# Transposed decay, update and attention matrices in a gated-delta-rule scan

## The reference

```python
decay = exp(where(incl, cum[:, None] - cum[None, :], -inf))
t_mat = where(strict, beta[:, None] * (k @ k.T) * decay, 0) + eye(c)      # I + L
sol   = triangular_solve(t_mat, [k * beta * exp(cum), v * beta])          # w_c, u_c
v_new = u_c - w_c @ s
o     = (q * exp(cum)) @ s + ((q @ k.T) * decay) @ v_new
s     = s * exp(cum[-1]) + (k * exp(cum[-1] - cum)).T @ v_new
```

## Time and profile before

| | before |
|---|---|
| median time | 2821.73 us |
| span of the profiled execution | 2811.5 us |
| busy: TensorE / VectorE / ScalarE / GpSimd | 2659.4 / 1589.4 / 1005.1 / 561.9 us |
| scan of layer 0 | from about 273 to 517 us of the span |
| scan of layer 1 | from about 1811 to 2033 us of the span |

### The profile page before, as it was taken

The page is one execution under the profiler, slowest core; times in us unless marked ns, Lnnn a source line. Parts: engine busy times, 40 slices in busy tenths (PEclk is TensorE's granted clock), DMA queues, the critical chain, the costliest instruction groups (busy, mean ns, idle before and its releaser), DMA issues.

```text
span 2811.5 us, 50275 instructions
## 1 busy us (share of the span) xinstructions
PE 2659.4 (95%) x21222; PEld 2123.3 (76%) x21222; DVE 1589.4 (57%) x2784; ACT 1005.1 (36%) x1642; POOL 561.9 (20%) x232
## 2 busy tenths in 40 slices
PE   7899999999999999999999989899899999999998
PEld 1388778888888888887787538777778787888676
DVE  4846677527554443435747764667637754352856
ACT  0335444322222343224532234454343333432542
POOL 0122000120113211321023512200031132242132
PEclk9999999999999999999999999999999999999999
DMA  8421000332222112220034552100053331231133
GB/s 261 150 69 44 20 23 22 108 116 98 79 87 90 61 53 100 80 91 27 31 120 147 194 190 75 46 26 25 25 186 114 101 109 57 92 125 61 35 117 116
DMA packets 95166, 250.97 MB, mean 89 GB/s; under 512 B 11010, under 2 KB 28804, under 8 KB 94432
## 3 DMA queue, kind: packets, MB, share of 16 engines
q1 hardware_dynamic: 84170, 219.56, 23.1%
q10 hardware_dynamic: 10774, 28.19, 2.8%
HBM read 205.12 MB, written 35.26 MB: 85 GB/s over the span
## 4 chain that ended last, share of the span: by engine, by line
PE 74%; DVE 15%; ACT 4%; issue 3%; DMA 3%; ACTq 0%; SPq 0%; DVEq 0%
PE ps L983 18%; PE ps L984 17%; PE ps L985 17%; PE ps L1570 4%; PE ps L991 4%; PE ps L1597 2%; PE ps L1000 2%; PE ps L1123 2%; DVE t_gcv L2280 1%; PE ps L1012 1%; DMA t_raw<-in_w_ada 1%; PE ps L1580 1%; PE ps L1077 1%; PE ps L1594 1%; PE ps L1169 1%
## 5 line engine op out<-in xcount | busy, mean ns | idle before, releaser
L944 POOL TENSOR_TENSOR t_wlo<-t_raw,t_whi 128x1024 fp32r<-128x1024 f32 x217 | 535.1, 2467 | 2178.5 <-ACT t_whi L1703 2178.5
L983 PE MATMUL ps<-t_u_hi,t_whi 128*128 128x512 f32 (+1 forms) x2368 | 862.6, 364 | 16.9 <-issue 5.4
L984 PE MATMUL ps<-t_u_lo,t_whi 128*128 128x512 f32 (+1 forms) x2368 | 834.4, 352 | 0.3 <-issue 0.3
L985 PE MATMUL ps<-t_u_hi,t_wlo 128*128 128x512 f32 (+1 forms) x2368 | 830.4, 351 | 0.0
L1703 ACT ACTIVATE t_whi<-t_raw 128x1024 fp32r<-128x1024 f32 x235 | 248.2, 1057 | 793.7 <-PE ps L985 680.2
L983 PEld LDWEIGHTS ps<-t_u_hi,t_whi 128*128 128x128 f32 x2368 | 449.6, 190 | 89.3 <-issue 19.7
L985 PEld LDWEIGHTS ps<-t_u_hi,t_wlo 128*128 128x128 f32 x2368 | 447.9, 189 | 63.5
L984 PEld LDWEIGHTS ps<-t_u_lo,t_whi 128*128 128x128 f32 x2368 | 449.7, 190 | 57.1 <-issue 3.3
L2903 DVE TENSOR_REDUCE t_amx<-ps 128x1 f32<-128x768 f32 (+1 forms) x120 | 101.5, 846 | 150.3 <-PE ps L1570 149.8
L1774 ACT ACTIVATE t_grp<-ps 128x512 f32<-128x512 f32 (+2 forms) x236 | 103.8, 465 | 221.4 <-PE ps L1000 103.0
L2280 DVE SCALAR_TENSOR_TENSOR t_gcv<-ps,t_par,t_gcv 128x511 f32<-128x511 f32 (+1 forms) x132 | 82.9, 628 | 106.1 <-ACT t_gcv L1774 102.1
(11 more groups left out here) (301 smaller groups left out, 3840.4 us busy)
## 6 DMA issues: line engine op xcount, KB each, us to landing
t_raw<-in_w_in SPq DMA_DIRECT2D x184, 512.0 KB, 3.6
t_raw<-in_w_ada SPq DMA_DIRECT2D x48, 512.0 KB, 4.5
t_raw<-in_w_br SPq DMA_DIRECT2D x32, 512.0 KB, 3.9
t_raw<-in_w_out SPq DMA_DIRECT2D x24, 512.0 KB, 4.4
t_sg<-gate_logits SPq DMA_DIRECT2D x28, 384.0 KB, 4.5
hs<-t_hstage ACTq DMA_DIRECT2D x20, 512.0 KB, 3.6
t_hring<-hs SPq DMA_DIRECT2D x20, 512.0 KB, 5.6
t_prob<-t_pT ACTq DMA_DIRECT2D x56, 128.0 KB, 2.1
```

Of the source, the lines that this page charges most:

```text
L944: pool.tensor_tensor(lo, raw[:, s % RAW, :], hi.bitcast(f32), ALU.subtract)\
L983: pe.matmul(o, lh, rh, start=first, stop=False)
L984: pe.matmul(o, lh, rl, start=False, stop=False)
L985: return pe.matmul(o, ll, rh, start=False, stop=last)
```

## The change

Everything that was formed as a matrix B is now formed as its transpose. The decay matrix, M and the attention matrix come out of the products in the orientation in which TensorE wants them as its stationary operand, and so `turn_m`, `turned_m` and the transposes of the attention matrix, with their copies, are gone. For this the factor beta goes to the columns: it is in the attention matrix and in k_tail, v enters unscaled (`beta_v` is gone), and q's norm moves from the attention matrix to the output (`within_chunk` on VectorE: one addition over 512 columns becomes four multiply-adds of 128 columns). `first_y` now fills Y with the masked copies and `first_x` transposes it into X; `first_q` waits for X. M, X and Y lie in two buffers in turn (`scan_m`, `scan_x`, `scan_y`). Two small VectorE operations a direction are added ahead of the scan.

```diff
+        def scan_m(t, d):
+            return grp[:, d, 2, :] if t % 2 else m_buf[:, d, :]
+        def scan_x(t, d):
+            return grp[:, d, 3, 256:512] if t % 2 else grp[:, d, 3, 0:256]
+        def scan_y(t, d):
+            return grp[:, d, 3, 0:256] if t % 2 else grp[:, d, 3, 256:512]
...
-                def turn_m():
-                    for d in range(2):
-                        ln.take("g_m")
-                        claim(3 * d)
-                        ln.done(turn(3 * d, m_buf[:, d, :]), "g_mt")
-                        lend("g_mt_ok", 3 * d)
-
-                def first_q():
+                def first_q(t):
                     for d in range(2):
-                        ln.take("g_mt_ok")
-                        ln.take("g_x0")
+                        ln.take("g_m")
+                        ln.take("g_y")
                         claim(3 * d + 1)
...
                 def within_chunk(d):
-                    ln.take("g_at_ok")
+                    ln.take("g_a")
...
-                            if t + 1 < NT:
-                                turn_m()
...
-                        if lv == 2:
-                            for d in range(2):
-                                if outs[d]:
-                                    ln.take("g_a")
-                                    claim(3 * d)
-                                    ln.done(turn(3 * d, grp[:, d, 0, :]), "g_at")
-                                    lend("g_at_ok", 3 * d)
...
-                def turned_m():
-                    for d in range(2):
-                        ln.take("g_mt")
-                        ln.done(run(grp[:, d, 2, :], ps[:, 3 * d, :], ACT.Copy), "g_mt_ok")
...
-                def beta_v(t):
...
                         for d in range(2):
-                            step(tt(dirs(gsc[:, 3, :], d), dirs(ec[:, 2 * d, :], d), dirs(gsc[:, 1, :], d), ALU.mult))
+                            step(ts(dirs(gsc[:, 3, :], d), dirs(ec[:, 2 * d, :], d), -1.0, None, ALU.mult))
+                            tail = dirs(ec[:, 2 * d + 1, :], d)
+                            step(tt(tail, tail, dirs(gsc[:, 0, :], d), ALU.mult))
...
-                def first_x(d):
+                def first_y(t, d):
                     ln.take("g_pre")
-                    x = by_head(grp[:, d, 3, 0:256])
+                    y = by_head(scan_y(t, d))
                     for r in near:
-                        last = dve.copy_predicated(x[r], over_heads(masks[r, d, 0, :]), by_head(m_buf[:, d, :])[r, :, r])
-                    ln.step(last, "g_x0")
-
-                def first_y(d):
-                    ln.done(dve.transpose(grp[:, d, 3, 256:512], grp[:, d, 3, 0:256]), "g_y")
+                        last = dve.copy_predicated(y[r], over_heads(masks[r, 1 - d, 0, :]), by_head(scan_m(t, d))[r, :, r])
+                    step(last)
+
+                def first_x(t, d):
+                    ln.done(dve.transpose(scan_x(t, d), scan_y(t, d)), "g_y")
...
                         ln.take("g_oa")
-                        ln.step(tt(gtok[:, c, :], ps[:, 6, :], gtok[:, c, :], ALU.add), "g_o2")
+                        ln.step(each(lambda h, s: stt(gtok[:, c, s], ps[:, 6, s],
+                                                      ssq[:, 2, c * HEADS + h:c * HEADS + h + 1],
+                                                      gtok[:, c, s], ALU.mult, ALU.add)), "g_o2")
...
                                 ln.take("g_ks")
-                                ln.take("g_pre")
                                 ln.done(each(lambda h, s: stt(grp[:, d, 0, s], ps[:, 3 * d + 2, s],
-                                                              gsc[:, 3, i0 + h:i0 + h + 1], grp[:, d, 0, s],
+                                                              gsc[:, 3, i0 + h:i0 + h + 1], vtok[:, c, s],
                                                               ALU.mult, ALU.add)), "g_r")
```

More of the change, by code:

```diff
@@ L1268, in decays @@
                         claim(3 * d)
-                        ln.done(pe.matmul(ps[:, 3 * d, :], cst[:, C_GE if d else C_LE, :], m_buf[:, d, :],
+                        ln.done(pe.matmul(ps[:, 3 * d, :], cst[:, C_LT if d else C_GT, :], scan_m(t, d),
                                           start=True, stop=True), "g_d")
@@ L1303, in gdn_scan @@
                 k_by_k(0)
-                turn_m()
-                first_q()
+                first_q(0)
                 for t in range(NT):
@@ L1314, in gdn_scan @@
                             claim(B + 1)
-                            ln.done(blocks(B + 1, grp[:, d, 2, :], grp[:, d, 3, :], d if lv == LEVELS - 1 else None, True,
-                                           lv),
+                            ln.done(blocks(B + 1, scan_m(t, d), scan_x(t, d), d if lv == LEVELS - 1 else None, True, lv),
                                     "g_q")
@@ L1334, in gdn_scan @@
                             ln.take("g_q_ok")
-                            ln.take("g_y")
+                            if lv > 1:
+                                ln.take("g_y")
                             if lv < LEVELS - 1:
                                 claim(B + 2)
-                                ln.done(blocks(B + 2, grp[:, d, 3, 256:512], grp[:, d, 5, :], lv=lv), "g_p")
+                                ln.done(blocks(B + 2, scan_y(t, d), grp[:, d, 5, :], lv=lv), "g_p")
                                 lend("g_x", B + 2)
@@ L1343, in gdn_scan @@
                             claim(B + 1)
-                            ln.done(blocks(B + 1, grp[:, d, 5, :], grp[:, d, 3, 256:512],
+                            ln.done(blocks(B + 1, grp[:, d, 5, :], scan_y(t, d),
                                            1 - d if lv == LEVELS - 1 else None), "g_pt")
@@ L1382, in gdn_scan @@
                     if t + 1 < NT:
-                        first_q()
+                        first_q(t + 1)
                     for d in range(2):
@@ L1961, in k_tail @@
                                 lambda h: ec[:, 2 * d + 1, c * 8 + d * 4 + h:c * 8 + d * 4 + h + 1], "g_ktail")
-                identities()
+                identities(0)
                 decays()
-                turned_m()
                 q_of(0, 1)
                 for t in range(NT):
-                    outs = [l == 0 or chunk(t, d) < LT for d in range(2)]
                     for lv in range(1, LEVELS):
@@ L1976, in gdn_scan @@
                         yield
[L1977 to L1981, removed]
                         if lv == 3 and t + 1 < NT:
@@ L2632, in gdn_scan @@
                             if lv <= IN_DVE:
-                                ln.step(dve.transpose(grp[:, d, 3, 256:512], grp[:, d, 3, 0:256]), "g_y")
+                                ln.step(dve.transpose(scan_y(t, d), scan_x(t, d)), "g_y")
                                 continue
@@ L2671, in gdn_scan @@
                         for d in range(2):
-                            first_x(d)
+                            first_y(t + 1, d)
                     for d in range(2):
-                        ln.take("g_vn")
+                        ln.take("g_yf")
                         if t + 1 < NT:
-                            first_y(d)
+                            first_x(t + 1, d)
                     if t + 1 < NT:
```

43 lines of the change are left out of this document (18 added, 25 removed).

## The result

Over seven runs each, the changed kernel took 2830.53 us (2825.14 to 2838.83), the kernel before 2817.49: a ratio of 1.0041, 95% interval 1.0026 to 1.0056. It is slower, where no change was forecast. The profiled execution took 2838.83 us, of which the span is 2837.0; it is the longest of the seven. In every run 1.7 to 2.3 us lie around the span, so of the 10.2 us that I put around the span of the kernel before, some 8 were the spread between executions.

A forecast was written before the change was run, and what follows sets the result against it. VectorE was taken to bound between state update and log decays, TensorE from there to the next state update. Terms +0.95 - 6.95 + 1.5 + 1.76 = -2.7 took the span from 2811.5 to 2808.8, 2819.0 with 10.2 around it; range 2811 to 2828.

The forecast's parts named there:

- the second unknown, the clock: TensorE's granted clock behind its waits in the scans: longer idle time, but no change taken in the count of half-clock falls.
- The third rival: Clock falls in all eight steps, twice each: ten stretches more at 1.5 us, a third hidden; +10, 2829; chance 0.20.
- The two waits and the transposes between them: TensorE's waits of 0.46 and 1.13 us at the attention transposes: old and new gap look the same to the clock gate.
- The attention transposes' steps: Ten groups of attention-matrix transposes removed, VectorE's queue 0.44 us longer per `within_chunk`: +0.95 us over ten steps, step 4 +0.9.
- M's transposes at level 6: Ten groups removed at level 6, 0.87 us mean each, partly limited by VectorE's right-hand side and `first_q`: -6.95 us.
- Start and end of a scan: Start: `first_q` waits for masked copies and transposes, +0.75 a layer; end: two `within_chunk` waits grow 0.44 each, +0.88 a layer.
- TensorE's busy time down by 20: Sign expected in the changed kernel: TensorE's busy time down by 20, its idle time up nearly as much.
- The sum without the clock, -2.7: All terms over the kernel, with no change in clock falls: +0.95 - 6.95 + 1.5 + 1.76 = -2.7 us.

The follow-up runs named there:

- the single addition: Changed kernel with `within_chunk` on VectorE as one addition of 512 columns, q's norm left out there: 2817.06 us, 0.9993 of the kernel before.
- q's norm late: Changed kernel with q's norm multiplied in behind the scan, within-chunk part added in one instruction: 2821.45 us, 1.0009; with discarded products at level 3 also, 2815.41 us, 0.9985.
- the spread run with fills: Changed kernel with VectorE's attention work spread over levels 2 and 3, discarded transposes in TensorE's waits: 2821.89 us, 1.0016 of the kernel before.

## Why the prediction was wrong

The failed step is the second unknown, the clock: "I take no change in the count". The count in the two scans went from 6 to 12, and the time at half clock from some 25 us to 71. The third rival, given 0.20, is what happened: its condition (the clock falls in each of the eight steps), its sign and its threshold (three more stretches). Its sum came out near for other reasons. It took ten stretches more of 3 us, two in each step (which would be eleven, 16 for 5); there is one in each step and six more in all, but up to 10 us long. It put +10 on the -2.7, so some +7 against the kernel before, and 2829 from a median of 2821.73 that became 2817.49 with more runs; the ratio of 1.0041 is 11.6 us (7.3 to 15.8).

- *The two waits and the transposes between them* were taken as worth no more to the clock than one wait of their sum. The run with the attention transposes put back refutes it: 1.0049 against 1.0019, with more work. The argument leaned on the Trainium skill's rule about transposes, and the run with transposes as fill refutes that as well. That a wait of this size can bring the clock down stood in the prediction, in the earlier trace rows and in the count of five falls in eight steps.
- *The attention transposes' steps*: right. Step 4 was to have its second q blocks at the end of VectorE's queue, 12.7 us behind the state update; they are at 12.70. The waits were to be some 2.5 and 0.6 us; they are 1.82 and 0.50.
- *M's transposes at level 6*: right. From the right-hand side to `g_vn` 3.30 us before (1845.04 to 1848.34) and 2.54 after, 0.76 less where 0.64 was taken; to `first_q` 5.87 before, 5.40 after, 0.47 less where 0.46 was.

```profile
1856.03 2.16 DVE L2254 SCALAR_TENSOR_TENSOR t_grp<-ps,t_gsc,t_acc 128x128 f32<-128x128 f32 x8 [1.99 <-PE ps L1003]
...
1858.57 2.05 PE L1003 MATMUL ps<-t_grp 128*128 128x128 f32 x16
...
1861.43 0.76 PE L1012 MATMUL ps<-t_grp 32*32 32x32 f32 x51
```

- *Start and end of a scan*: right in kind and nearly in size. At the start `first_q` ends 9.66 us behind the start of the first sum instead of 8.67: +0.99, part of it at half clock, for +0.75. (Its old end is 282.01 by the earlier trace rows, where the prediction has 281.94.) At the end both waits grew from 0.95 to 1.38, 0.43 each for 0.44.

```profile
285.81 0.98 PE L1012 MATMUL ps<-t_grp,t_oT 32*32 32x32 f32 x64 [3.96 <-issue]
...
521.38 1.13 PE L1003 MATMUL ps<-t_grp 128*128 128x128 f32 x8 [1.38 <-DVE t_gtok L2254]
...
523.89 0.47 PE L995 MATMUL ps<-t_u_hi,t_whi 128*128 128x512 f32 x1 [1.38 <-DVE t_gtok L2254]
```

- *"TensorE's busy time down by 20"*: wrong, and by the same step as far as the scans go: there it fell by 0.4, since what runs at half clock is busy up to twice as long. The rise of 10.2 over the whole lies outside the scans (2209.54 to 2220.23), with the remainder below.
- *The sum without the clock, -2.7*: not settled to its size. With the wait filled the ratio is 1.0000 (0.9986 to 1.0013), which holds -2.7 and also +3, and the fill takes some time itself. The part of it that the four multiply-adds cost depends on the clock. With products in the wait, taking q's norm out of the scan makes the scans 3.8 us shorter (496.03 to 492.19); without a fill the single addition made them 10.8 shorter, of which half clock accounts for 3 at most. The sum is near the first of these prices, and the kernel paid the second.
- *Outside the scans* the profiled run after is 15.8 us longer than the one before, with only small operations changed ahead of the scan; by the runs' medians the whole difference is 13.0, and 9.75 of it lies in the two scans. Over all profiled runs that part takes 2311.7 to 2332.5 us, with 2316.75 before and 2332.5 after at the end of it, so one profile can't say whether the change has any part in it. I can't show a cause for the remainder. The ratios of the experiments hold it too, which is why the table has the scans beside them.

What half clock costs: between the changed kernel run again and the same with products in the wait, some 51 us less of it are worth 6.8 us in the scans, 0.13 us for each, with the fill's own place in it. With q's norm late it is 5.4 us for 41, 0.13 again; in the kernel before with products 4.3 for some 15, 0.28. The prediction had 1.5 us for a stretch of 3, a third hidden, 0.33. More is hidden than a third, and I take the reason to be that TensorE there is at the end of VectorE's queue anyway, which no run parts. That the total came out near is owed to more time at half clock (some 46 us more for the rival's 30) at a smaller price, and to a queue that costs more in the kernel whose clock falls: the rival has the mechanism right and is lucky in the sum.

## What to carry to other kernels

A wait has a second price beside its length: what it does to the clock of the work behind it. Removing work from the middle of a wait can be slower than leaving it there. So before you cut short operations that stand between two waits of an engine near its bound, look in the granted clock at what those waits do already, and price the case in which the joined wait is a fall in every pass. Price what the change adds to the queue of the engine that is waited for as well; here either of the two alone undid the gain. If a fall can't be avoided by moving real work into the wait, discarded work cut to end before the wait does is worth trying; in this kernel the fill that was longer kept the clock as well and was slower.

## What the runs showed of the hardware

- Single waits of 1.82 to 3.18 us in each step, between stretches of small block products, came with 1.2 GHz in or behind them in all five steps of layer 0 that have output before them. With the wait split by transposes, mostly into 0.47 and 1.13 us, there were falls in three of the five (transposes put back) and four of the five (the kernel before).
- Transposes of 128 columns hold TensorE's clock as products do: 1.0008 and 1.0000 of the time before, with 1.00 granted in all four steps between the first and last state update of layer 0.
- VectorE's masked copies of 64 partitions, 1.84 us for both directions, took 3.72 us in the step of the spread run with fills where GpSimd's split of a weight tile (2.37 us) began 0.33 us earlier, and 3.74 in the same step with transposes as fill:

```profile
1924.59 2.37 POOL L956 TENSOR_TENSOR t_wlo<-t_raw,t_whi 128x1024 fp32r<-128x1024 f32 x1 [33.24 <-ACT t_whi L1706]
1924.92 3.72 DVE L2572 COPY_PREDICATED t_grp<-t_masks,t_grp 64x256 f32<-64x256 uint8 x4 [0.60 <-ACT t_grp L1777]
```
